# The opening of a streaming encoder layer in column halves: the scale's first half, then four chunks begun over half of the features

## The chip, the cores and the metric

One NeuronCore of a Trainium2 chip runs the whole program. The metric is the device time of one launch in microseconds. PE is TensorE, DVE VectorE, ACT ScalarE, POOL GpSimd, SP SyncE, whose queue issues nearly all large transfers.

## What is computed

One layer over 256 prompt tokens and 32 sample tokens of 1024 features, in float32. The scale and the shift come from a conditioning vector `c` of each of the two groups of tokens.

```python
sh1, sc1, g1, sh2, sc2, g2 = silu(c) @ w_ada + b_ada          # 6 x 1024 columns
h = rms_norm(x, norm1_g) * (1.0 + sc1) + sh1
proj = h @ w_in                                                # 512 pool, 512 conv value, 512 conv gate
a = pool_mix(proj[:512]);  u = proj[512:1024] * sigmoid(proj[1024:1536])
b = silu(layer_norm(depthwise_conv31(u))) @ conv_w_out
gates = sigmoid(h @ gate_w + gate_b)                           # 2048 columns
x = x + g1 * ((gates[:1024] * a + gates[1024:] * b) @ w_out)
h2 = rms_norm(x, norm2_g) * (1.0 + sc2) + sh2
x = x + g2 * moe_top4_of_32(h2)                                # three 1024x1024 matrices per expert
y = rms_norm(x, final_g)
```

## The kernel before

Each engine has one program written out by hand; semaphores order them. Nothing is scheduled by a planner: what stands earlier in an engine's text runs earlier.

**Weights of the front.** The list `FRONT` names pieces of 1 MB. SP issues them in that order (L454) into a ring of 12 slots; piece f waits for `piece_used` to reach f - 11, and PE counts that semaphore up when it has finished with a piece. The pieces in order are four of the scale, two of `w_in`, four of the shift, four more of `w_in`, then gates and the other modulation columns, and the pool, convolution and output weights. The three transfers of the tokens go ahead of all; the last of them is issued at 1.70 us.

**The opening.** `x` is squared on ACT in three tiles (L629), the root is taken (L632), DVE scales the tiles (L856), PE transposes them feature block by feature block (L1362, `turn_x`, eight in all) and DVE copies each block of 128 features to `hS` (L859). Beside it PE computes the modulation: `first_rows` (L1331) puts the bias into a bank, `first_half` (L1341) multiplies one piece, that is two feature blocks by all 1024 columns, in four products of 512 columns. Each of these takes 32 partitions of the bank, that is one strip of 32 columns of the array. ACT copies the finished bank to `rows` (L634), `to_columns` (L1352) turns it to columns, DVE makes `scc` and multiplies `hS` by it (L888). `fill` (L1320) is a product of the identity with ones whose result is never read.

**Projection.** It has 12 chunks of 128 columns, each a sum over 8 feature blocks (L1423, 128x288). The first four (`UNSHIFTED`) are taken before the shift is known: two of the convolution's gate and two of its value. The shift's own products (L1445) are added to their banks afterwards (L1464, through `group_of`), and `hT` (L900) is the shifted input of all others. In L1451 to L1459 the taps and the stored rows are transposed. Two gate and two value chunks are enough for tiles 0 and 1 of the depthwise convolution, which DVE runs as 31 taps per tile (L918 forms the product, L929 and L932 are the taps).

**Gates and after.** 16 gate chunks (L1476) alternate with products of the remaining modulation columns (L1397). The layer norm's mean and variance are taken in after gate chunks 6 and 8 (`MEAN_AT`, `VAR_AT`). Then pool, convolution and output products follow (L1526, L1546, L1563), and the router.

**Experts.** SP loads each expert in six pairs of slots (2 MB each); nine pairs are filled ahead, the last of them once `h2` is ready, and from the tenth on a load waits until PE is done with the pair it replaces (L493, issued in L460). An item is up to 64 tokens of one expert; 33 items run in this profile. An item begins with the gate product (L1690), 16 products that each stand as two records in the trace. Ahead of the first item PE passes the router's tables and two `fill(1)` calls.

## Time and profile before

| | |
|---|---|
| median of three runs | 1157.67 us (1156.29 to 1159.33) |
| profiled execution | 1158.99 us, its span 1157.1 us |
| PE busy | 1128.9 us (98%) |
| DVE busy | 500.3 us (43%) |
| ACT busy | 177.5 us (15%) |
| DMA share of 16 engines, ring and expert weights | 94.4% |
| HBM read | 454.40 MB, 394 GB/s over the span |

The profiled execution takes 1.9 us more than its span, for what lies around the recorded instructions. Busy time of PE is modelled and says little of how well it is used. The chain of work that ended last is followed back from the last instruction; its pieces are printed in order of time with start and length, so a piece that starts where the one before it ends leaves no hole. Clock is shown as a share of 2.4 GHz, so 0.50 is 1.2 GHz.

### The profile page before, as it was taken

The numbers are of one execution on the slowest core, as the hardware profiler recorded it, in microseconds if no ns is written. First come the engines' busy times: TensorE is split into PE (matmuls) and PEld (weight loads), VectorE is DVE, ScalarE is ACT, GpSimd is POOL, SyncE is SP. The second block draws the span as 40 slices with busy tenths as digits, with TensorE's granted clock in tenths as the row PEclk, the third lists the DMA queues.
The fourth block names the chain that finished last, engine by engine and source line by source line (L and its number), as shares of the span: only waits on it lengthen the run. The fifth ranks groups of instructions, "written<-read, shape, count | busy, mean of one in ns | idle before, by whom it ended". The sixth has DMA issues, their size and how long they took to land.

```text
span 1157.1 us, 16132 instructions
## 1 busy us (share of the span) xinstructions
PE 1128.9 (98%) x5964; PEld 459.7 (40%) x5965; DVE 500.3 (43%) x1143; ACT 177.5 (15%) x333; POOL 29.5 (3%) x78
## 2 busy tenths in 40 slices
PE   9999999999999999999999999999999999999996
PEld 6676675633333333333322333333333333333332
DVE  3398524654333443344333443344334433333334
ACT  2001301311111111111111112111111111111112
POOL 4002300000000000000000000000000000000000
PEclk9999999999999999999999999999999999999998
DMA  9977699699999999999999999999999999999994
GB/s 348 373 278 273 251 299 321 217 368 428 428 428 428 428 430 428 428 428 430 428 428 428 429 428 428 428 429 428 429 427 429 428 429 429 428 427 429 428 428 195
DMA packets 58012, 456.13 MB, mean 394 GB/s; under 512 B 7125, under 2 KB 26385, under 8 KB 31237
## 3 DMA queue, kind: packets, MB, share of 16 engines
q1 hardware_dynamic: 53872, 452.35, 94.4%
q10 hardware_dynamic: 4117, 3.47, 1.3%
q8 instruction: 16, 0.26, 0.1%
q14 instruction: 7, 0.06, 0.0%
HBM read 454.40 MB, written 1.40 MB: 394 GB/s over the span
## 4 chain that ended last, share of the span: by engine, by line
PE 78%; DMA 21%; DVE 1%; issue 0%; POOL 0%; DVEq 0%; SPq 0%; POOLq 0%
PE bank L1690 46%; DMA ring<-in_exp_w_up 7%; DMA ring<-in_exp_w_gate 7%; PE bank L1476 5%; PE bank L1423 4%; PE bank L1717 4%; PE bank L1642 4%; DMA arena<-in_exp_w_up 3%; DMA arena<-in_exp_w_gate 3%; PE bank L1563 2%; PE bank L1772 1%; PE bank L1546 1%; PE bank L1650 1%; PE bank L1397 1%; PE bank L1708 1%; PE bank L1320 1%
## 5 line engine op out<-in xcount | busy, mean ns | idle before, releaser
L1690 PE MATMUL bank<-ring,arena 128*64 128x512 f32 x2112 | 472.5, 598 | 11.3 <-DMA ring<-in_exp_w_gate 10.1
L1690 PEld LDWEIGHTS bank<-ring,arena 128*64 128x64 f32 x2112 | 146.9, 137 | 313.6 <-issue 286.5
L1690 PE MATMUL bank<-arena 128*64 128x512 f32 x1056 | 236.1, 595 | 5.3 <-DMA arena<-in_exp_w_gate 5.1
L1690 PEld LDWEIGHTS bank<-arena 128*64 128x64 f32 x1056 | 73.3, 137 | 155.5 <-issue 137.9
L780 ACT ACTIVATE arena<-arena 32x256 f32<-32x256 f32 x136 | 56.0, 412 | 422.8 <-DVE arena L1163 421.6
L1247 DVE TENSOR_SCALAR arena<-bank 128x512 f32<-128x512 f32 x33 | 22.8, 691 | 168.0 <-PE bank L1690 168.0
L1254 DVE TENSOR_SCALAR arena<-bank 128x512 f32<-128x512 f32 x33 | 22.8, 691 | 167.8 <-PE bank L1690 167.8
L1232 DVE TENSOR_TENSOR x<-x,bank 128x512 f32<-128x512 f32 x132 | 84.5, 681 | 13.0 <-PE bank L1717 13.0
L1269 DVE TENSOR_TENSOR arena<-bank,biases 128x512 f32<-128x512 f32 x66 | 42.5, 685 | 110.2 <-PE bank L1690 110.2
L793 ACT ACTIVATE arena<-arena 128x512 f32<-128x512 f32 x33 | 20.8, 629 | 356.7 <-DVE arena L1247 356.7
L1717 PE MATMUL bank<-arena 64*128 64x512 f32 x264 | 65.6, 615 | 0.0
L1476 PE MATMUL bank<-arena,ring 128*128 128x288 f32 x256 | 64.4, 409 | 0.0
L1642 PE MATMUL bank<-h,arena 128*64 128x512 f32 x268 | 63.3, 592 | 0.0
L932 DVE SCALAR_TENSOR_TENSOR h<-h,arena 128x318 f32<-128x318 f32 x120 | 55.5, 537 | 0.0
L1476 PEld LDWEIGHTS bank<-arena,ring 128*128 128x128 f32 x256 | 48.1, 190 | 17.1 <-issue 4.2
L1423 PE MATMUL bank<-arena,ring 128*128 128x288 f32 x192 | 47.7, 408 | 0.0
L793 ACT ACT_TABLE_LOAD x33 | 42.3, 1283 | 0.6
L1423 PEld LDWEIGHTS bank<-arena,ring 128*128 128x128 f32 x192 | 36.1, 190 | 11.4 <-issue 1.7
L1654 PE MATMUL bank<-biases,mine 32*64 32x288 f32 x264 | 40.0, 414 | 0.0
L1717 PEld LDWEIGHTS bank<-arena 64*128 64x128 f32 x264 | 22.7, 186 | 42.3 <-issue 42.3
L1168 DVE COPY arena<-arena 32x256 f32<-32x256 f32 x136 | 38.4, 282 | 2.5
L1651 PE MATMUL bank<-biases,mine 32*64 32x512 f32 x136 | 37.4, 613 | 0.0
(306 smaller groups left out, 742.8 us busy)
## 6 DMA issues: line engine op xcount, KB each, us to landing
ring<-in_exp_w_down SPq DMA_DIRECT2D x43, 2048.0 KB, 28.9
ring<-in_exp_w_up SPq DMA_DIRECT2D x43, 2048.0 KB, 28.8
ring<-in_exp_w_gate SPq DMA_DIRECT2D x42, 2048.0 KB, 28.1
arena<-in_exp_w_gate SPq DMA_DIRECT2D x22, 2048.0 KB, 26.4
arena<-in_exp_w_up SPq DMA_DIRECT2D x21, 2048.0 KB, 28.7
arena<-in_exp_w_down SPq DMA_DIRECT2D x20, 2048.0 KB, 30.3
ring<-in_w_ada SPq DMA_DIRECT2D x24, 1024.0 KB, 9.9
ring<-in_gate_w SPq DMA_DIRECT2D x8, 1024.0 KB, 7.8
```

What stands on the lines that cost most here:

```text
L780: ins = a.activation(*square_moves(1, s, u), ACT.Copy)
L793: a.activation(gsig, gmin, ACT.Sigmoid, scale=ALPHA).then_inc(gsig_ready, 1)
L932: ins = v.scalar_tensor_tensor(out=yc[:, c, :], in0=uc_ext[:, c, k:k + CW], scalar=tap, in1=yc[:, c, :], op0=ALU.mult, op1=ALU.add)
L1168: ins = v.tensor_copy(*square_moves(0, s, u))
L1232: ins = v.tensor_tensor(x[:, t, cs], x[:, t, cs], scatter_bank(t, hh), ALU.add)
L1269: v.tensor_tensor(ysb[:, gg, :], bank[5][:, :], g2h[:, gg, :], ALU.mult).then_inc(y_ev, 1)
L1423: ins = mm(bank[n % 4][:, 0:TOK], w[:, k, P * (n % 2):P * (n % 2 + 1)], (hS if n < UNSHIFTED else hT)[:, k, :], start=(k == 0), stop=(n >= ...
L1476: ins = mm(bank[n % 4][:, 0:TOK], w[:, k, P * (n % 2):P * (n % 2 + 1)], hT[:, k, :], start=(k == 0), stop=(k == KD - 1))
L1642: ins = mm(bank[0][64 * hh:64 * hh + 64, :], oh[:, t, :], half_rows(h2[:, t, :], hh), start=start, stop=stop, skip_group_check=True)
L1654: found = mm(bank[6 + i][out, 0:TOK], mine[LOOKUP, :], routedT[:, i, :], start=True, stop=True, skip_group_check=True)
L1690: ins = mm(out[64 * hh:64 * hh + 64, :], lhs(k), w[:, D * (k % 2) + HALF * hh:D * (k % 2) + HALF * (hh + 1)], start=(done is y_mm and k == ...
L1717: ins = mm(scatter_bank(t, hh), ohwT[64 * hh:64 * hh + 64, P * t:P * (t + 1)], ysb[64 * hh:64 * hh + 64, 0, :], start=True, stop=True, ski ...
```

## The change

**Pieces.** A scale or shift piece is now four feature blocks by 512 columns, named (kind, half of the columns, half of the features). A `w_in` piece is four feature blocks by 512 columns, so two pieces hold four chunks. The order is: both pieces of the scale's first 512 columns, the first `w_in` piece, the two of the scale's second half, the second `w_in` piece, four of the shift, four of `w_in`.

**Tokens.** ACT squares tiles 0 and 1 before anything else, DVE squares and sums tile 2 (32 rows). Then ACT scales tile 1 and DVE tiles 0 and 2. The sigmoid of `c` comes after that on ACT, with its table.

**PE.** The first four blocks of the tokens are transposed before any modulation product. The first scale half is made, turned to columns and applied to features 0 to 511. Then the four unshifted chunks, all gates of the convolution now, run over those features, with the second scale half between them; then the same four run over the other features, with the shift between them. Each half has its own bank (4 and 5), its own `first_rows` and its own `to_columns`. ACT copies blocks 4 to 7 to `hS` where DVE did.

**Later.** Chunk 4 is the first that gives the convolution a value. Taps run six alone for tile 0, then six for tile 1 (`ALONE`), then both in turn as before. `MEAN_AT` and `VAR_AT` go from 6 and 8 to 8 and 10; the modulation rows leave after gate 11 for 9, and two small copies on DVE move up. The two fills ahead of the first item become `fill(2)` and `fill(5)`.

```diff
-FRONT = ([("scale", 0, j) for j in range(4)] + [("in", c, 0) for c in (4, 2)]
-         + [("shift", 0, j) for j in range(4)] + [("in", c, 0) for c in (5, 3, 0, 1)]
+FRONT = ([("scale", 0, 0), ("scale", 0, 1), ("in", 2, 0), ("scale", 1, 0), ("scale", 1, 1), ("in", 2, 1)]
+         + [("shift", h, j) for h in range(2) for j in range(2)] + [("in", c, j) for c in (1, 0) for j in range(2)]
...
-MEAN_AT, VAR_AT, STATES_AT = 6, 8, 10
+MEAN_AT, VAR_AT, STATES_AT = 8, 10, 10
...
+            a.activation(stat[:, 31:32], stat[:, 30:31], ACT.Sqrt)
+            for t in range(2):
+                act.wait_ge(x_ld[t], 16)
+                a.activation(view(2304 + D * t, D), x[:, t, :], ACT.Square, accum_out=stat[:, t:t + 1]).then_inc(ssq, 1)
+            act.wait_ge(mean2, 1)
+            a.activation(stat[:, 4:7], stat[:, 8:11], ACT.Sqrt).then_inc(sqrt_ready, 1)
+            act.wait_ge(rstd0_ready, 1)
+            a.activation(h2[:, 1, :], x[:, 1, :], ACT.Copy, scale=stat[:, 5:6]).then_inc(xn_ready, 1)
             act.wait_ge(c_cols_ready, 1)
             a.activation(csig[:, :], c_cols[:, :], ACT.Sigmoid).then_inc(csig_ready, 1)
...
+            for k in range(4, KD):
+                act.wait_ge(xT, k + 1)
+                a.activation(hS[:, k, :], bank[k % 4][:, 0:TOK], ACT.Copy).then_inc(xT_act, 1)
...
+            dve.wait_ge(x_ld[2], 16)
+            step(v.tensor_tensor(squares, x[0:NS_TOK, 2, :], x[0:NS_TOK, 2, :], ALU.mult))
+            step(v.tensor_reduce(stat[0:NS_TOK, 2:3], squares, AX, ALU.add))
...
-            glu((0, 1))
+            glu((0,))
+            dve.wait_ge(u_ready, 1)
+            dve.wait_ge(dw_ready, 1)
+            conv((0,), 0, ALONE)
+            glu((1,))
             dve.wait_ge(u_ready, 2)
-            dve.wait_ge(dw_ready, 1)
-            conv((0, 1), 0, CONV_SPLIT)
+            conv((1,), 0, ALONE)
+            conv((0, 1), ALONE, CONV_SPLIT)
...
-            first_rows(2)
-            fill(3)
-            pe.wait_ge(cT_ready, 1)
-            fill(4)
-            first_half("scale", 0)
-            fill(6)
-            first_half("scale", 1)
+            first_rows(2, bank[4])
+            fill(12)
+            pe.wait_ge(xn_ready, TT)
+            for k in range(4):
+                turn_x(k)
...
+            pe.wait_ge(cT_ready, 1)
+            first_half("scale", 0, 0)
+            first_half("scale", 0, 1)
             turn_x(4)
-            fill(2)
-            first_half("scale", 3)
             turn_x(5)
+            pe.wait_ge(pick_made, 2)
+            to_columns(0, 0)
             turn_x(6)
-            pe.wait_ge(pick_made, 2)
-            to_columns(0)
             turn_x(7)
+            pe.wait_ge(cols_ready, 1)
+            first_rows(3, bank[5])
             fill(2)
...
+            for n in range(UNSHIFTED):
+                pe.wait_ge(xT_act, n + 1)
+                chunk(n, 0)
+                if n < 2:
+                    first_half("scale", 1, n)
+                elif n == 2:
+                    to_columns(0, 1)
+            first_rows(0, bank[4])
+            first_rows(1, bank[5])
+            for n in range(UNSHIFTED):
+                chunk(n, 1)
+                first_half("shift", n // 2, n % 2)
+                if n == 3:
+                    to_columns(1, 0)
+                    to_columns(1, 1)
+
+            pe.wait_ge(shift_ready, 2)
...
-            fill(1, bank[1])
+            fill(2, bank[1])
             pe.wait_ge(begun_ready, 1)
...
-            fill(1, bank[1])
+            fill(5, bank[1])
             pe.wait_ge(base_ready, 1)
```

How the order of instructions moves, at two places. First PE, from the last fill ahead of the first projection chunk: before, whole chunks in a row.

```order
L1320 MATMUL bank<-ones,ident 128x128 x2
L1423 MATMUL bank<-arena,ring 128x288 x16
L1331 MATMUL bank<-arena 32x512 x2
L1341 MATMUL bank<-ring,cT 32x512 x8
L1423 MATMUL bank<-arena,ring 128x288 x8
L1341 MATMUL bank<-ring,cT 32x512 x8
L1423 MATMUL bank<-arena,ring 128x288 x4
L1352 MATMUL bank<-arena 128x4 x4
L1423 MATMUL bank<-arena,ring 128x288 x4
L1445 MATMUL bank<-ring,arena 32x256 x16
```

The same place with the change (`first_rows` is now L1341, `first_half` L1348, `to_columns` L1360, the chunks L1417):

```order
L1341 MATMUL bank<-arena 32x512
L1331 MATMUL bank<-ones,ident 128x128 x2
L1417 MATMUL bank<-arena,ring 128x288 x4
L1348 MATMUL bank<-ring,cT 32x512 x4
L1417 MATMUL bank<-arena,ring 128x288 x4
L1348 MATMUL bank<-ring,cT 32x512 x4
L1417 MATMUL bank<-arena,ring 128x288 x4
L1360 MATMUL bank<-arena 128x4 x4
L1417 MATMUL bank<-arena,ring 128x288 x4
L1341 MATMUL bank<-arena 32x512 x2
L1417 MATMUL bank<-arena,ring 128x288 x4
L1348 MATMUL bank<-ring,cT 32x512 x4
```

Four products, half a chunk, now stand between pieces of the modulation, columns are turned between them, and the bias row of the scale's second half stands ahead of the first chunk.

Second DVE, where the depthwise convolution starts: before, both tiles' products first, then the taps of both in turn.

```order
L918 TENSOR_TENSOR h<-bank,arena 128x256
L918 TENSOR_TENSOR h<-bank,arena 128x32
L918 TENSOR_TENSOR h<-bank,arena 128x256
L918 TENSOR_TENSOR h<-bank,arena 128x32
L929 TENSOR_SCALAR h<-h,arena,cols 128x318 x2
L932 SCALAR_TENSOR_TENSOR h<-h,arena 128x318 x34
```

The same place with the change (L924 forms the product, L935 and L938 are the taps):

```order
L924 TENSOR_TENSOR h<-bank,arena 128x256
L924 TENSOR_TENSOR h<-bank,arena 128x32
L935 TENSOR_SCALAR h<-h,arena,cols 128x318
L938 SCALAR_TENSOR_TENSOR h<-h,arena 128x318 x5
L924 TENSOR_TENSOR h<-bank,arena 128x256
L924 TENSOR_TENSOR h<-bank,arena 128x32
L935 TENSOR_SCALAR h<-h,arena,cols 128x318
L938 SCALAR_TENSOR_TENSOR h<-h,arena 128x318 x29
```

Tile 0 now has its product and six taps (one in L935, five in L938) ahead of tile 1's product.

## Rows read from the trace of the kernel before

**Rows 1.** The page, section 4: shares of the chain that ended last

```profile
PE 78%; DMA 21%; DVE 1%; issue 0%; POOL 0%; DVEq 0%; SPq 0%; POOLq 0%
```

**Rows 2.** The chain in order of time, opening: start us, us, what

```profile
13.76 0.99 PE bank L1341 x8
...
15.81 2.02 PE bank L1362 x12
...
22.09 0.98 PE bank L1352 x8
...
23.52 0.64 PE bank L1320 x4
24.17 7.87 PE bank L1423 x32
32.04 0.98 PE bank L1331 x4
33.01 1.85 PE bank L1341 x16
34.87 4.08 PE bank L1423 x16
...
40.80 2.14 PE bank L1423 x8
42.94 0.79 PE bank L1352 x8
43.72 2.05 PE bank L1423 x8
45.77 1.86 PE bank L1445 x32
...
48.49 2.14 PE bank L1464 x8
```

**Rows 3.** The chain of the whole program: chunks, first item, late experts

```profile
50.63 31.04 PE bank L1423 x128
...
230.85 9.79 PE bank L1690 x32
...
243.12 7.02 PE bank L1690 x32
...
1001.72 40.33 DMA ring<-in_exp_w_up
```

**Rows 4.** Windows: length, PE, PEld, DVE, ACT, POOL busy, PEclk, DMA share, GB/s

```profile
230.00:231.00 1.00, 0.23 (x3) 0.16 (x4) 0.88 (x5) 0.96 (x3) 0.00 (x0) 0.50 1.07 459
...
237.00:238.00 1.00, 1.00 (x8) 0.39 (x6) 0.24 (x3) 0.00 (x0) 0.00 (x0) 1.00 0.04 16
```

**Rows 5.** Timeline of SP's queue: start us, us, engine, line, transfer

```profile
237.24 0.33 SPq L460 DMA_DIRECT2D ring<-in_exp_w_up  x1
```

**Rows 6.** Timeline of the opening, ACT and DVE; last row: landing of the tokens

```profile
4.24 1.28 ACT L623 ACT_TABLE_LOAD   x1 [4.24 <-issue]
...
8.03 1.04 ACT L629 ACTIVATE arena<-x 128x1024 f32<-128x1024 f32 x1
...
11.27 0.17 DVE L835 TENSOR_SCALAR stat<-stat 128x3 f32<-128x3 f32 x1 [4.45 <-ACT arena L629]
...
11.92 2.07 DVE L856 TENSOR_SCALAR h<-x,stat 128x1024 f32<-128x1024 f32 x3
...
DMA to landing us min/median/max: 3.3/4.6/5.3
```

**Rows 7.** Timeline of DVE, later: a reduce and a product of 1024 columns

```profile
109.00 2.39 DVE L947 TENSOR_REDUCE arena<-h 128x318 f32<-128x1272 f32 x1
...
202.02 1.21 DVE L1051 TENSOR_TENSOR h<-h,arena 32x1024 f32<-32x1024 f32 x1
```

**Rows 8.** Timeline of DVE where the convolution begins

```profile
50.35 0.95 DVE L918 TENSOR_TENSOR h<-bank,arena 128x256 f32<-128x256 f32 x4 [2.03 <-ACT arena L659]
...
52.05 8.37 DVE L932 SCALAR_TENSOR_TENSOR h<-h,arena 128x318 f32<-128x318 f32 x18
```

More of the change, by code:

```diff
@@ L419, in build @@
         ada_piece = {(a, b): f for f, (kind, a, b) in enumerate(FRONT) if kind == "ada"}
+        piece_of = {piece: f for f, piece in enumerate(FRONT)}
         pool_stage = [biases[0:POOL_PAD, 0, 0:DC], biases[0:CONV_PAD, 0, DC:D]]
@@ L637, in _ @@
             act.dma_start(dw_stage, conv_dw[0]).then_inc(dw_ld, 16)
+            act.wait_ge(ada_mm, 2)
+            a.activation(rows[:, 1, :], bank[5][:, :], ACT.Copy).then_inc(rows_ready, 1)
             act.dma_start(pool_stage[0], state_pool[0, 0]).then_inc(st_ld, 16)
             act.dma_start(pool_stage[1], state_conv[0, 0]).then_inc(st_ld, 16)
-            act.wait_ge(ada_mm, 2)
-            a.activation(rows[:, 1, :], bank[4][:, :], ACT.Copy).then_inc(rows_ready, 1)
+            act.wait_ge(ada_mm, 3)
@@ L642, in _ @@
+            a.activation(rows[:, 0, :], bank[4][:, :], ACT.Copy).then_inc(rows_ready, 1)
+            act.wait_ge(ada_mm, 4)
+            a.activation(rows[:, 1, :], bank[5][:, :], ACT.Copy).then_inc(rows_ready, 1)
             act.wait_ge(shift_mm, 1)
@@ L866, in _ @@
+            scale_half(0)
+            scale_half(1)
+            v.memset(uc_ext[:, :, 0:CONV_PAD], 0.0).then_inc(hist0_ready, 1)
             dve.wait_ge(const, 7)
             v.reciprocal(invc[:, :, :], invc[:, :, :]).then_inc(mod_ready, 1)
-            def columns(at):
-                return bank[7][:, at:at + 16].rearrange("p (r j g) -> p j r g", r=4, j=2)
-            four = "p (j r g) -> p j r g"
-            dve.wait_ge(modT, 1)
-            for gg in range(2):
-                v.scalar_tensor_tensor(out=scc[:, :].rearrange(four, j=2, g=2)[:, :, :, gg], in0=columns(0)[:, :, :, gg],
-                                       scalar=1.0, in1=cols[:, C_N1:C_N1 + KD].rearrange("p (j r) -> p j r", j=2),
-                                       op0=ALU.add, op1=ALU.mult).then_inc(mod_ready, 1)
@@ new lines, in _ @@
+            pe.wait_ge(shift_ready, 2)
+            for k in range(KD):
+                q = k % 4
+                ins = mm(bank[4][32 * q:32 * q + 32, :], shT[:, k, :], front_piece(piece_of[("in", 2, k // 4)])[1][:, k % 4, :],
+                         start=(k < 4), stop=(k >= 4), skip_group_check=True)
+            ins.then_inc(shift_mm, 1)
+            pe.wait_ge(cols_ready, 1)
+            pe.wait_ge(dw_ld, 16)
+            for c in range(CT):
+                ins = tr(bank[5][:, 32 * c:32 * c + WIDTH], dw_stage[:, P * c:P * (c + 1)], ident[0:WIDTH, 0:WIDTH])
+                if c == 0:
+                    ins.then_inc(piece_used, 8)
@@ new lines, in _ @@
+            ins.then_inc(dwT, 1)
+            pe.wait_ge(st_ld, 32)
+            for c in range(CT):
+                tr(bank[6][:, 32 * c:32 * c + POOL_PAD], pool_stage[0][:, P * c:P * (c + 1)], ident[0:POOL_PAD, 0:POOL_PAD])
+            for c in range(CT):
+                ins = tr(bank[6][:, 128 + 32 * c:128 + 32 * c + CONV_PAD], pool_stage[1][:, P * c:P * (c + 1)],
+                         ident[0:CONV_PAD, 0:CONV_PAD])
+            ins.then_inc(stT, 1)
+            pe.wait_ge(shift_ev, 1)
@@ L1467, in _ @@
+            for m in range(UNSHIFTED):
+                mm(bank[m][:, 0:TOK], rows[:, 2, P * m:P * (m + 1)], group_of, start=False, stop=True,
+                   skip_group_check=True).then_inc(in_mm, 1)
+            for n in range(UNSHIFTED, 12):
+                if n < 8:
+                    pe.wait_ge(sig_ready, n - 3)
+                else:
+                    pe.wait_ge(u_ready, n - 7)
+                chunk(n, 0)
+                chunk(n, 1).then_inc(in_mm, 1)
             for n in range(2 * KD):
```

244 lines of the change are left out of this document (91 added, 153 removed).

## Prediction, made before the changed kernel ran

> **What bounds the kernel now.** I read the page's shares of the chain first, then the chain in order of time, then clock and DMA in short windows, then DVE and ACT where the change touches them.
>
> The page gives 78% of the chain that ended last to PE and 21% to DMA [rows 1]. In order of time these are two regimes. From 13.76 us on the chain is PE without a hole: each piece starts where the one before it ends, and the eight projection chunks from 50.63 on take 31.04 us in one piece [rows 2, 3]. Where PE had to wait, small identity products ("fills") stand in the chain, as at 23.52, so a wait there reads as PE work. In the second regime, the experts, the chain ends in DMA: one weight half ends 40.33 us of it [rows 3]. The two are tied. Nine pairs of slots are filled ahead, and the tenth transfer waits until the first item has used pair 0. So the end comes a fixed stream of transfers after that first use, unless the DMA engines are still busy with the pairs ahead. They just weren't: their traffic fell to 16 GB/s at 237 to 238 us, and the tenth transfer was issued at 237.24 [rows 4, 5].
>
> Hence: what the opening gains or loses on PE arrives at the first item, and from there at the end, nearly one to one. The sum is made against the profiled execution, 1158.99 us; the median of the three runs is 1157.67, so that execution lies 1.32 above it. A measurement of this kernel can tell about 0.3%, here 3.5 us, from no change: faster means under 1154.2, slower over 1161.1.
>
> **When the tokens' transposes can start.** Before: the normalised tokens were there at 11.92 + 2.07 = 14.0, but PE, with two scale pieces ahead of them, came at 15.81 [rows 2, 6]. Now ACT loads its root table first (1.28 from 4.24) and squares two tiles, 1.04 each [rows 6]: 5.5, its root of one element 0.2, then 5.75 to about 8.05. DVE squares the third tile once it has landed, 1.70 + 5.3 = 7.0 [rows 6]. The square costs 1.21 by the row of a 32x1024 operation; the sum of 1024 elements I bound by that row and by the 2.39 of the reduce over 1272 elements [rows 7], and take 1.5, since it has fewer elements and reads them in order: 9.8. From mean to first scaled tile took 11.92 - 11.27 = 0.65 [rows 6]; two tiles remain on DVE, 2 x 0.7, ACT does the third beside them. That gives 11.9 to 12.8; I take **12.5**, 3.3 earlier than 15.81.
>
> **PE from there to the fifth chunk.** Terms, with the rows of group 2:
> - Eight transposed blocks 2 x 2.02 (four at 15.81) = 4.1 with the sum's rounding up, the small table 0.2: as before.
> - The first scale half, two pieces together as 1.85, was half done before the transposes and is now behind them.
> - Columns of the scale: 0.98. The bias row of the other half, a lone 512-column product: the row at 32.04 has two in 0.98, but in different column strips of the array, and four in four strips also take 0.99 (13.76). So 0.98 is the time of one, not of two. Bounds 0.49 and 0.98; I take 0.9. Two fills 0.3 each.
> - First chunk at 12.5 + 4.1 + 0.2 + 1.85 + 0.98 + 0.9 + 0.6 = **21.1**, against 24.17. Its cover is good: the row copy on ACT (0.6) lies beside two transposes.
> - Eight half chunks at 2.1 (2.14 at 40.80) = 16.8; before, the four chunks took 7.87 + 4.08 + 2.14 + 2.05 = 16.1, as a product that follows another kind pays some 0.15.
> - Six pieces one at a time 6 x 0.99 = 5.9, where four stood in pairs (1.85 each).
> - Columns again 0.8, and twice in a row 1.7 (0.79 to 0.98 each): there are four such steps where there were two.
> - Two bias rows, now in two banks but the same strip: 1.8, where they were side by side in 0.98.
> - The wait for the shift's columns, until now covered by half a chunk (43.72 stands behind 42.94), is open: copies on DVE, 0.4.
> - Shift products 1.86 (eight of 512 for sixteen of 256), stored rows and taps 48.49 - 47.63 = 0.86, shift added 2.14: as before.
>
> 21.1 + 16.8 + 5.9 + 0.8 + 1.7 + 1.8 + 0.4 + 1.86 + 0.86 + 2.14 = **53.4**, against 50.63: **2.8 later**. The first chunk comes 3 us sooner, and the path behind it has grown by nearly 6, two of them the second scale half that is carried past it, the rest steps that are now split, repeated or uncovered.
>
> **DVE.** The convolution began beside chunk four (50.35, [rows 8]) because its two operands were among the first four chunks. Now all four first chunks are gates, so it begins 3.9 + 0.3 after chunk four starts. Tile 0 alone takes six taps, each waiting for the last: 5 x 0.6 + 0.4; the same for tile 1; then 24 at 8.37 / 18 = 0.465 [rows 8]. The third product is ready 23.6 after the chunk began, and chunk ten, which needs its bank, could start at 6 x 3.88 = 23.3 (3.88 is 31.04 / 8). I charge **0.4**. Everything behind comes some 7 us later relative to PE; the mean and the variance were moved two gates later each (about 10 us), which covers it, and the activation for the output is then due some 12 us after it is ready. Cost nothing.
>
> **DMA.** The ring's early releases are now later and coarser: two before the taps' transposes, then eight at once. After the tokens (7.0 us) 14 pieces of 1.05 MB take 37 us at the page's 394 GB/s; then the queue is dry from 44 to the taps' transposes at 50.4, some 6 us. The first gate piece is needed 31 us later and takes a few: nothing. The weight pieces arrive before PE asks for them, since PE asks later.
>
> **The clock at the first item.** Ahead of 230.85 PE has only the small products of the router's tables, two single fills and a gap (busy 0.23 of the window from 230); the granted clock has fallen to 0.50 there, 1.2 GHz, and reads 1.00 again from 237 [rows 4]. The first product takes 9.79, the next like it 7.02 [rows 3]. Pair 0 comes free half a product in, at 16 x 0.4 instead of 16 x 0.22 us: 2.9 late, of which the idle DMA shows 2.0, and a half us more at the next transfers. The change raises these two fills to two and five, five more, 5 x 0.3 = 1.5 us by the two of them in 0.64 [rows 2]. Bounds of the gain: 0 (clock falls all the same) and 2.5 (stays up); against the gain at most 0.3, as the next work queues behind them. Taken: 2.2 gained, 0.2 paid, because the five stand exactly where the fall began.
> The Trainium skill (TensorE: Matmul & The Clock Gate, section "Why this matters for your kernels") asks that PE not be left idle between bursts. By that rule alone nothing here asked for a fall, since the gap is under 1 us, and more fills would give nothing: the end would be 1162.4. The trace differs: the clock fell.
>
> Sum: 1158.99 + 2.8 + 0.4 + 0.2 - 2.2 = **1160.2 us**.
>
> **Rivals.**
> - *The clock falls all the same.* Place: the first product of the first item. For it: the router's small products stay as they are, and more fills may not hold the clock. Price: 2.2 back, 1162.4, slower. It decides as soon as less than 1.3 of the 2.2 is won. Chance 0.33.
> - *PE's list is not additive.* The 0.15 at each change of kind, the lone bias rows and the extra column steps may slip beside their neighbours, as weight loads do. Then the half chunks cost 15.7, bias rows 1.5 in all, columns 0.5 each: 53.4 - 1.1 - 1.2 - 1.5 = 49.6, and the end is 1156.4. For it: PE is never idle in rows whose busy time is modelled. Against it: the same switches in the rows of before all cost this. Chance 0.17; a third of it, with a first use earlier than the pairs' landing and a short reduce, goes below 1154.2.
> - *The tokens come late.* If squares or landing of the third tile drag (reduce 2.39, tile at 8), transposes start at 14 and PE idles 1.5 before them: 1161.7, and with a clock that falls in that hole, 2 more. Chance 0.1.
> - *The half-column order does not matter*, since the steps taken up by fills before are merely renamed and the fifth chunk starts at 50.6 again: 1157.4. Chance 0.05.
>
> **Numbers.** Forecast 0.35, clock 0.33, the others as given. Below 1154.2 lie a third of the second rival's 0.17 and 0.02 of the forecast's own spread (1158.5 to 1162): 0.08. Over 1161.1 lie 0.27 of the clock's case, 0.07 of the late tokens' and 0.06 of that spread: 0.4; between, 0.52. The range takes in the clock's case and 0.9 us above it, 1163.3, and below it the second rival's 1156.4 and 0.4 more: 1156.0.
>
> **What would show it.** First half chunk at 21 (right if 20.5 to 22), first of the eight unbroken chunks at 53.4 (52.4 to 54.4), bias rows about 1.8 for two, the first item at 234. Windows behind it: clock near 1.00 and first product near 7. The second rival's case shows the fifth chunk before 51. I am wrong in kind if PE waits for a weight piece anywhere before 230, if DVE holds chunk ten by more than 1 us or the gates at all, or if the end does not follow the first item.

## The result, and the profile after

The change made the kernel slower by about half a per cent: 1162.88 us, median of 8 runs (1161.26 to 1165.71), against 1157.74 for the kernel before in the same job (8 runs, 1154.32 to 1159.33). The ratio is 1.0053 with a 95% interval of 1.0041 to 1.0064. The forecast was 1160.2, within 0.3% of before; the time lies inside the range, at its upper end, and outside "same".

The profiled execution of the changed kernel took 1161.58 us, its span is 1159.6. The shares of the chain that ended last, page section 4, answer to [rows 1] and hardly moved:

```profile
PE 76%; DMA 21%; DVE 2%; issue 0%; ACTq 0%; DVEq 0%; SPq 0%
```

The two points of DVE are new. The chain in order of time (start us, us, what) answers to [rows 2, 3] and shows where they come from (`...` marks pieces left out):

```profile
8.29 4.29 PE bank L1331 x24
12.59 2.02 PE bank L1370 x12
...
17.74 0.99 PE bank L1360 x8
...
19.71 0.97 PE bank L1341 x2
...
21.33 3.59 PE bank L1417 x8
24.92 1.00 PE bank L1348 x8
25.91 2.14 PE bank L1417 x8
...
34.02 1.83 PE bank L1341 x4
...
48.38 1.89 PE bank L1360 x16
...
50.39 0.17 DVE arena L900
...
50.61 1.92 PE bank L1442 x16
...
53.39 2.14 PE bank L1461 x8
55.52 3.89 PE bank L1417 x16
...
78.92 8.03 PE bank L1417 x32
86.95 7.76 PE bank L1481 x32
...
234.87 1.31 PE bank L1331 x10
...
236.28 7.09 PE bank L1695 x32
```

The transposes start at 12.59, 3.2 earlier than before, and the first half chunk at 21.33, 2.8 earlier. From there the path is longer: the fifth chunk starts at 55.52, 4.9 later than before. The first half chunk takes 3.59 where every later one takes 2.14 or 2.05. Chunk ten waits for the convolution on DVE (the chain runs over DVE from 59.4 to 78.9), so the gate stage follows the start of the fifth chunk after 31.43 us and not 31.04.

The windows (length, PE, PEld, DVE, ACT, POOL busy, granted clock, DMA share, GB/s) give the reason for the 3.59 and show the place of [rows 4]:

```profile
22.00:23.00 1.00, 1.00 (x4) 0.71 (x3) 0.00 (x0) 0.00 (x0) 0.00 (x0) 0.50 1.04 383
23.00:24.00 1.00, 1.00 (x3) 0.71 (x3) 0.00 (x0) 0.00 (x0) 0.00 (x0) 0.50 1.05 389
...
25.00:26.00 1.00, 1.00 (x9) 0.16 (x3) 0.00 (x0) 0.00 (x0) 0.00 (x0) 1.00 1.04 375
...
236.00:237.00 1.00, 0.90 (x6) 0.35 (x6) 0.86 (x5) 0.98 (x3) 0.00 (x0) 1.00 1.12 475
237.00:238.00 1.00, 1.00 (x6) 0.30 (x4) 0.85 (x5) 0.98 (x1) 0.00 (x0) 1.00 0.96 410
```

The clock was at its lower level, 1.2 GHz, from about 21.5 to 24.9, straight behind the transposes, pieces and columns, although PE's rows show it busy throughout 19 to 25. At the first item it now stays at 1.00, and DMA has no gap: 410 GB/s at 237 to 238, where [rows 4] have 16. The tenth transfer was issued at 239.97, against 237.24 in [rows 5]:

```profile
239.97 0.33 SPq L463 DMA_DIRECT2D ring<-in_exp_w_up  x1
```

From that issue to the end of the span it is 919.6 us here and 919.9 before. So the profiled difference is settled at this point: 2.7 later, 2.6 longer.

One thing at the very start the windows don't show. They print 1.00 for all time ahead of the trace's first clock record, and that record lies at 11.2 us here and at 11.1 in the kernel before, but at 4.9 to 6.2 in the profiles of e2, e4, e5, e7, e8, e9, e11 and e12 below. Ahead of it PE's rows take about twice as long: a lone bias row 1.91 at 6.38 against 0.97 at 19.71, and the twelve fills from 8.29 on 4.29 against some 2.9 in those eight. So PE presumably ran at the lower level until then, and when that ends differs between executions. It decides here when the fills end and the transposes begin.

The tokens, on DVE and ACT, which answer to [rows 6, 7]:

```profile
7.22 1.21 DVE L847 TENSOR_TENSOR arena<-x 32x1024 f32<-32x1024 f32 x1 [0.86 <-DMA x<-in_x_sample]
...
8.46 1.21 DVE L848 TENSOR_REDUCE stat<-arena 32x1 f32<-32x1024 f32 x1
...
10.36 1.15 ACT L633 ACTIVATE h<-x,stat 128x1024 f32<-128x1024 f32 x1 [0.24 <-DVE stat L852]
10.36 1.40 DVE L856 TENSOR_SCALAR h<-x,stat 128x1024 f32<-128x1024 f32 x2
```

### The profile page after: what moved, and what is told of

Same layout as the page of the kernel before. It is cut to its first block, busy times and chain, and to the rows that moved or that the text cites. A ratio compares the mean times of both kernels' runs of the same rounds, so it can differ in the third digit from the quotient of the medians.

```text
span 1159.6 us, 16138 instructions
## 1 busy us (share of the span) xinstructions
PE 1131.6 (98%) x5962; PEld 460.5 (40%) x5963; DVE 501.3 (43%) x1142; ACT 178.9 (15%) x336; POOL 30.3 (3%) x80
## 4 chain that ended last, share of the span: by engine, by line
PE 76%; DMA 21%; DVE 2%; issue 0%; ACTq 0%; DVEq 0%; SPq 0%
PE bank L1695 45%; DMA ring<-in_exp_w_up 7%; DMA ring<-in_exp_w_gate 7%; PE bank L1481 5%; PE bank L1722 4%; PE bank L1647 4%; DMA arena<-in_exp_w_up 3%; DMA arena<-in_exp_w_gate 3%; PE bank L1417 3%; PE bank L1568 2%; PE bank L1777 1%; DVE h L938 1%; PE bank L1551 1%; PE bank L1655 1%; PE bank L1401 1%; PE bank L1713 1%
## 5 line engine op out<-in xcount | busy, mean ns | idle before, releaser
L1243 DVE TENSOR_TENSOR x<-x,bank 128x512 f32<-128x512 f32 x132 | 84.5, 681 | 12.6 <-PE bank L1722 12.6
L1481 PE MATMUL bank<-arena,ring 128*128 128x288 f32 x256 | 64.4, 409 | 0.0
L938 DVE SCALAR_TENSOR_TENSOR h<-h,arena 128x318 f32<-128x318 f32 x120 | 56.3, 536 | 0.4
L1417 PE MATMUL bank<-arena,ring 128*128 128x288 f32 x192 | 50.7, 420 | 0.1
L1417 PEld LDWEIGHTS bank<-arena,ring 128*128 128x128 f32 x192 | 36.6, 194 | 15.2 <-issue 5.0
L1661 PE MATMUL bank<-h,arena 32*64 32x512 f32 x136 | 37.4, 613 | 0.0
```

Source lines behind the costliest of these rows:

```text
L938: ins = v.scalar_tensor_tensor(out=yc[:, c, :], in0=uc_ext[:, c, k:k + CW], scalar=tap, in1=yc[:, c, :], op0=ALU.mult, op1=ALU.add)
L1243: ins = v.tensor_tensor(x[:, t, cs], x[:, t, cs], scatter_bank(t, hh), ALU.add)
L1417: ins = mm(bank[n % 4][:, 0:TOK], w[:, k % 4, P * (n % 4):P * (n % 4 + 1)], (hS if n < UNSHIFTED else hT)[:, k, :], start=(k == 0), stop=( ...
L1481: ins = mm(bank[n % 4][:, 0:TOK], w[:, k, P * (n % 2):P * (n % 2 + 1)], hT[:, k, :], start=(k == 0), stop=(k == KD - 1))
```

## What was to be told apart

Profile against profile the change cost 2.6 us. The clock in one half chunk is 1.65 of it: the first half chunk took 3.59, and 1.94 at full clock (e2, e10 and e11 below). The medians are 5.1 apart: the profiled execution of before lay 1.3 above its median and that of after 1.3 below. Two theories:

- **A.** The list of steps on PE is priced rightly, and the rest is the clock: the new opening puts small products in longer stretches, with waits of PE among them, and loses the clock there in many executions. The mean granted clock of a run tells how long it was down after the first clock record: 0.001 of 1160 us is 2.3 us at half speed, or 1.2 us of PE's work not done.
- **B.** The list is dear in itself (column steps, bias rows, single pieces), and the clock is a detail of one execution.

Each kernel below ran in 5 rounds beside the kernel before, and its ratio to that is what counts: the median of before was 1156.45 in the first job of e1 to e4, 1157.64 for e5 to e8, 1157.57 for e9 and e10, 1158.2 for e11 and e12.

## The fills ahead of the first item

**e1, the kernel before with the two fill counts of the change, nothing else.**

```diff
-            fill(1, bank[1])
+            fill(2, bank[1])
...
-            fill(1, bank[1])
+            fill(5, bank[1])
```

> The kernel before with only the last edit of the change: two and five fills ahead of the first item instead of one and one. Theory (the fills hold the clock at the first item): the first product takes about 7.1 us instead of 9.79, the tenth weight transfer is issued some 2.7 us sooner, and the median is 1 to 2.5 us under that of the kernel before. Rival (the clock at the first item is chance, the fills do nothing): first product near 9.8 or 7 by luck, median within 0.5 us of before.

**e2, the change with these fills put back to one each** (the same diff the other way).

> The changed kernel with one and one fill again. Theory: the first product is near 9.8 us again with a granted clock of 0.50 at it, and the median rises by 1 to 2.5 us over the changed kernel's 1162.9. Rival: no difference, 1162.9 within 0.5.

Measured: e1 1154.94 (12 runs), ratio 0.9987 [0.9977, 0.9997]; e2 1164.85 (6 runs), 1.0084 [1.0061, 1.0106]. The first item in the chain of e1, and below it in that of e2:

```profile
232.40 7.09 PE bank L1690 x32
```

```profile
236.79 8.78 PE bank L1695 x32
```

The clock in e2's windows there:

```profile
236.00:238.00 2.00, 1.21 (x4) 0.45 (x6) 1.79 (x9) 1.95 (x5) 0.00 (x0) 0.75 0.96 410
238.00:240.00 2.00, 2.00 (x6) 0.51 (x4) 1.73 (x10) 0.92 (x1) 0.00 (x0) 0.50 1.07 459
```

With seven fills the first product took 7.09 in eleven of the twelve profiles that have them; with two it took 9.79 (before) and 8.78 (e2, where the clock fell only as the product began). The twelfth is e8, below: its clock was down from 238.3 to 251.9 in spite of seven fills.

```profile
248.93 8.52 PE bank L1691 x32
```

So the fills make the fall there rare, not impossible. They are the one part of the change that was seen to gain over the kernel before: 1.5 us by e1's median and ratio, and 2.0 (medians) to 3.6 (ratios) between e2 and the change. So the opening by itself costs more than the result shows: 1.0053 / 0.9987 is 1.0066, 7.6 us, and e2, which is the opening without the fills, measured 1.0084, 9.7 us, with an interval that takes in both.

e1 also shows scatter that the mean clock doesn't tell. Its twelve runs all read 0.997 or 0.998 and spread over 3.3 us. In its profile the fifth chunk started at 51.89, 1.26 later than in that of before, with the windows at 1.00 in both; the first clock record lay at 13.8 instead of 11.1, and the pieces before it took up to twice as long.

## Parts of the opening

**e3, bias rows of the two halves in two strips of the array.**

```diff
-                mm(out[0:32, :], ada_sel[:, row, :], bada[:, :], start=True, stop=False, skip_group_check=True)
+                mm(out[32 * (row % 2):32 * (row % 2) + 32, :], ada_sel[:, row, :], bada[:, :], start=True, stop=False, skip_group_check=True)
...
-                             start=(j == 0 and q > 0), stop=(j == 1), skip_group_check=True)
+                             start=(j == 0 and q != h), stop=(j == 1), skip_group_check=True)
```

> The changed kernel, but the bias row of each second half goes to the second strip of 32 partitions instead of the first, so that the two bias rows of the shift stand in different strips. Theory (a lone 512-column product takes as long as four in four strips, and two in one strip are serial): the pair takes 0.98 us instead of 1.83, everything behind comes 0.85 sooner, median 1162.0. Rival (the pair is bound by its bank or its issue): still 1.8, median unchanged.

Measured: 1164.16 (6 runs), 1.0078 [1.0058, 1.0099]. The pair of bias rows in the chain of e3:

```profile
33.80 0.98 PE bank L1341 x4
```

1.83 has become 0.98, and the fifth chunk of the profiled execution starts 1.06 earlier, at 54.46; that execution took 1160.19. The median didn't follow. The six runs are spread over 1160.19 to 1168.83, with clocks from 0.987 to 0.996: the 0.85 is real in the profile, and lost in the scatter of the clock.

**e4, the token blocks turned by products with the identity instead of transposes.** Values are the same.

```diff
-                    ins = tr(bank[k % 4][:, P * t:P * t + r], h2[0:r, t, P * k:P * (k + 1)], ident[0:r, 0:r])
+                    ins = mm(bank[k % 4][:, P * t:P * t + r], h2[0:r, t, P * k:P * (k + 1)], ident[0:r, 0:r], start=True, stop=True)
```

> The changed kernel with the 24 transposes of the tokens made as ordinary products with the identity. It tests what lets the clock fall at the first half chunk (0.50 from 21.7 to 24.9 us in the changed kernel's profile). Theory A (transposes do not hold the clock): the clock stays at 1.00 through the first half chunk, which takes 2.1 us instead of 3.59; median 1.5 us lower if that happens in most runs. Theory B (it is the thin products, four columns and four rows, between them, or where the clock's own rhythm falls): 3.6 again, or 2.1 with no change of the median. If a product costs more than a transpose, the eight blocks take over 4.1 us.

Measured: 1169.42 (5 runs), 1.0112 [1.0092, 1.0133]. Chain, then a window, of e4:

```profile
11.55 6.08 PE bank L1370 x24
```

```profile
13.00:15.00 2.00, 2.00 (x10) 1.71 (x8) 0.64 (x3) 0.00 (x0) 1.48 (x8) 0.50 1.06 389
```

Twice the records, at half clock: 6.08 for what took 2.02. So the fall isn't bound to transposes as a kind. Real products of this size, with PE busy 2.00 of 2.00 us, stood in it from 12.7 to 22.9, and the clock was down again from 26.3 to 33.2. But PE had waited 1.6 us for the tokens just ahead of these products, so this execution alone doesn't tell the wait from the products.

**e5, the last two token blocks turned later, each behind a half chunk.**

```diff
-            turn_x(6)
-            turn_x(7)
...
                 if n < 2:
+                    turn_x(6 + n)
                     first_half("scale", 1, n)
```

> The changed kernel with the last two transposed blocks moved from ahead of the first half chunk to behind the first and the second one. Nothing is added. Theory (after the half-column order PE has 4.7 us of transposes, four-column products and a lone bias row in one stretch, and there the clock falls): the stretch is 3.7 us, the first half chunk starts 1 us sooner (about 20.3), the start of chunk four gains little (the blocks cost the same behind it), but falls are rarer: mean granted clock of the runs over the changed kernel's 0.9946 mean, median about 1 us lower. Rival (falls come by the clock's own rhythm, wherever PE is): clock and median as in the changed kernel.

Measured: 1163.58 (6 runs), 1.0075 [1.0047, 1.0103]. Chain of e5:

```profile
19.93 3.56 PE bank L1415 x8
...
49.96 3.29 PE bank L1441 x16
```

The first half chunk comes 1.4 sooner, half of it because the transposes began 0.7 sooner, and is as slow as in the change. A second place appears: the shift products took 3.29 instead of 1.92. One microsecond less of small work ahead of the chunk did not keep the clock, and the mean clock of the runs came out lower than the change's, 0.992, where the theory had it higher.

**e6, two wide products (128 x 512) in the stretch, one of them for the two last fills.**

```diff
+            def wide():
+
+                mm(bank[6][:, :], ident[:, :], ring[:, 1, 0:HALF], start=True, stop=True)
+
...
+            wide()
             to_columns(0, 0)
...
-            fill(2)
+            wide()
```

> The changed kernel with a full 128x128 by 512 product whose result is not read put behind the sixth transposed block, and another in the place of the two short fills before the first half chunk. Cost by the list: 0.85 + 0.25 = 1.1 us of PE ahead of the first half chunk (it starts at about 22.4). Theory (long products hold the clock): no fall at the first half chunk, it takes 2.1 us instead of 3.59; the granted clock of the runs reads 0.997 or so and they scatter by less; median equal to the changed kernel's or up to 1 us lower. Rival: falls as before, median 1.1 us higher.

Measured: 1164.57 (6 runs), 1.0066 [1.005, 1.0083]. Chain, then a window, of e6:

```profile
21.19 2.00 PE bank L1366 x2
23.20 2.64 PE bank L1422 x8
```

```profile
22.00:24.00 2.00, 2.00 (x5) 1.06 (x4) 0.00 (x0) 0.00 (x0) 0.00 (x0) 0.50 1.05 385
```

The fall came all the same: the first wide product took 1.06, the second, at the lower clock, 2.00. They did not keep the clock, and the mean clock is that of the change (0.9947 for 0.9946). Their own time is 1.7 us by the medians, for 1.1 expected, though the intervals of the two ratios overlap.

**e8, the tokens handled as before (sigmoid first, all squares on ACT, all scaling on DVE), with the new order on PE.** The part on the squares:

```diff
-            for t in range(2):
+            for t in range(TT):
+                r = ROWS[t]
                 act.wait_ge(x_ld[t], 16)
...
-            step(v.tensor_tensor(squares, x[0:NS_TOK, 2, :], x[0:NS_TOK, 2, :], ALU.mult))
-            step(v.tensor_reduce(stat[0:NS_TOK, 2:3], squares, AX, ALU.add))
```

> The changed kernel with the tokens handled as before: sigmoid first, all three tiles squared on ACT, all three scaled on DVE; PE's order unchanged. Theory (the transposes start when the scaled tokens are there): they start at about 14.2 instead of 12.6, and PE is idle between its fills and then; everything behind is 1.6 us later plus what a fall of the clock in that hole costs; median 1164.5 to 1167. Rival (pieces of the scale bound the opening, so the tokens' order is hidden): within 0.5 us of the changed kernel.

**e10, e8 with 17 fills for 12 ahead of the transposes.**

> The version with the tokens' squares back on ACT (e8), whose transposes stood at half clock from 14.04 on, with 17 fills instead of 12 ahead of the transposes, so that the time from 12.6 to 14.0 in which PE waited for the tokens is filled. Theory A (that idle time dropped the clock, and the late tokens by themselves cost only 1.5 us): transposes from about 14.1 at full clock (x12 in 2.0, not 3.5), first half chunk at 22.7 to 23.5, median 1164 to 1166 (ratio 1.005 to 1.007). Theory B (the thin work from 12 to 22 us loses the clock whether PE waited before it or not): transposes 3.5 again, first half chunk after 28, median near e8's 1169.

Measured: e8 1169.26 (6 runs), 1.0094 [1.0069, 1.012]; e10 1163.97 (6 runs), 1.0061 [1.0042, 1.0081]. e8 is over the 1164.5 to 1167 that were expected, and its profiled execution, 1175.65, is the slowest of its six. PE's timeline of e8 (in brackets the wait ahead and what ended it), then a window:

```profile
7.31 2.94 PE L1327 MATMUL bank<-ones,ident 128*128 128x128 f32 x24
14.04 3.51 PE L1366 MATMUL bank<-ident,h 128*128 128x128 f32 x12 [3.79 <-DVE h L858]
```

```profile
16.00:22.00 6.00, 6.00 (x26) 1.82 (x25) 1.35 (x4) 0.55 (x1) 1.04 (x4) 0.50 1.05 387
```

The same places in e10, windows and chain:

```profile
12.00:14.00 2.00, 2.00 (x12) 2.00 (x12) 1.99 (x3) 0.00 (x0) 1.86 (x2) 1.00 1.05 387
...
16.00:22.00 6.00, 6.00 (x43) 3.35 (x43) 2.17 (x10) 1.86 (x5) 1.05 (x4) 1.00 1.05 387
```

```profile
14.72 2.02 PE bank L1366 x12
```

Five small fills gave back 5.3 us by the medians, 3.8 by the ratios, whose intervals overlap. Between the two profiles the first half chunk starts 6.1 us sooner, at 23.47 instead of 29.53, although the transposes began 0.7 later. In e8 PE stood idle from 10.25 to 14.04, 3.8 us and not the 1.4 that the expectation of e10 names; the clock fell at 13.0, inside this wait, and stayed at 1.2 GHz for 20.5 us. In e10 there was no wait. Part of this is the start again: e10's first clock record lies at 13.7, and its 17 fills took 6.74. At the pace of e8's fills they would end some 2.5 us before the tokens (estimate: 34 records at 2.94 / 24), so the five fills don't close the wait in every execution; the mean clock of the six, 0.9962 for 0.989, is what says that they mostly work. This is the strongest effect of the study. Filled, the late tokens cost little: e10's ratio is 0.0008 over that of the change, 0.9 us, and the two intervals overlap.

The other half of the distance between these two profiles, 5.4 of 11.8 us, arose between the gate stage and the tenth transfer, where e8 lost the clock a second time (238.3 to 251.9). Whether the late tokens had a part in that is not shown.

## A leaner list, and the second place

**e7, all of it together:** strips as e3, late blocks as e5, the bias row and the small tables moved to where nothing waits for them, and the convolution's taps in turn end at 16 instead of 18.

```diff
-ALONE, CONV_SPLIT = 6, 18
+ALONE, CONV_SPLIT = 6, 16
...
             for k in range(4):
                 turn_x(k)
+            first_rows(3, bank[5])
...
-            to_columns(0, 0)
-            turn_x(6)
-            turn_x(7)
             pe.wait_ge(cols_ready, 1)
-            first_rows(3, bank[5])
+            to_columns(0, 0)
```

> The changed kernel with four costs of its opening taken away: the late two transposed blocks of the other run, the scale's second bias row made at the start beside the first (0.97 off the path), the shift's two bias rows in different strips (0.85), and 16 instead of 18 taps ahead of the second pair of products (0.4, the hold of the eleventh chunk, goes). Theory (PE's list is additive): chunk four starts 1.8 us sooner than with the same clock, 2.2 in all at the first item; against the changed kernel's profile of 1161.58 that is 1159.4, or 1157.8 if the clock does not fall at the first half chunk. The kernel before with its better fills, 1154.9, still is not reached. Rival (the list is not additive, waits for pieces or the tokens come in): less than 1 us gained.

Measured: 1159.06 (12 runs), 1.0021 [1.001, 1.0032]. Its chain:

```profile
18.34 2.18 PE bank L1415 x8
...
30.41 0.98 PE bank L1341 x4
...
46.14 3.41 PE bank L1441 x16
...
52.68 31.04 PE bank L1415 x128
```

3.8 us less than the change, by the medians and between the two profiles; the steps that were taken out sum to 2.2. The profiles tell where the 3.8 are: 1.64 because the transposes began sooner (10.95, first clock record at 5.5), 1.20 between them and the fifth chunk, 0.39 for the hold of chunk ten (the eight chunks are in one piece of 31.04 again), 0.56 behind the tenth transfer. Of the 1.82 expected up to the fifth chunk (bias row 0.97, strips 0.85), 1.2 came, with about the same loss by the clock in both (1.65 in the half chunk there, 1.63 at the shift here): with the bias row and two blocks gone, PE waited 0.49 for the scaled features. So the list is additive until such a wait opens, and that the profile met the 1157.8 expected for a kept clock (1157.78) is luck. The shift products stood at half clock, directly behind PE's wait for the columns. Two edits of that place:

**e9, the two column steps of the shift with half of a half chunk behind each.** The new third argument of `chunk` picks feature blocks.

```diff
             for n in range(UNSHIFTED):
-                chunk(n, 1)
+                if n < 3:
+                    chunk(n, 1)
                 first_half("shift", n // 2, n % 2)
-                if n == 3:
-                    to_columns(1, 0)
-                    to_columns(1, 1)
+            to_columns(1, 0)
+            chunk(3, 1, slice(0, 2))
+            to_columns(1, 1)
+            chunk(3, 1, slice(2, 4))
```

> The leaner version (e7) with one more edit: the last half chunk (four gate chunks' last, 2.14 us) is cut in two and put between the two column steps of the shift, the last shift piece before them. Nothing is added. The wait for the shift's column copies (0.34) is covered again, so the gate chunks should start 0.3 to 0.5 earlier relative to the first half chunk (65.4 after it in e7's profile, so 64.9 to 65.1), less if the clock falls. Theory A (the clock falls at about 46 to 53 us because last piece, two column steps, shift products, transposes of taps and states stand in one stretch of small products, some 7 us long, and before that there was a half chunk inside it): the shift products take 1.9 instead of 3.4, the mean clock of all runs rises from e7's 0.9956 to 0.997 or more, and the median is 1.5 to 2.5 under e7's (ratio to before about 0.999 to 1.001). Theory B (the falls come with time and chance and are not bound to that stretch): the median is 0.3 to 0.5 under e7's (ratio 1.001 to 1.002) and the shift products take 3.4 in the profile again.

**e12, e7 with three fills ahead of the wait.**

```diff
+            fill(3)
             pe.wait_ge(shift_ready, 2)
```

> The leaner version (e7) with three fills ahead of the wait for the shift's column copies, where PE stood for 0.35, and nothing else: the stretch of small products stays as long as in e7. Theory A (the wait decides): shift products 1.9 instead of 3.4 in the profile, fifth chunk 1.5 to 2 earlier than in e7 relative to the first half chunk (34.3 there, so 32.3 to 32.9), median 1 to 1.5 under e7's (ratio 1.0005 to 1.001), as e9. Theory B (the length of the stretch decides): shift products 3.4 again, median e7's or up to 0.3 over it (ratio 1.002 to 1.0025).

Measured: e9 1158.05 (12 runs), 1.0007 [0.9994, 1.002]; e12 1158.86 (12 runs), 1.001 [1.0, 1.0021]. Chain of e9, then of e12:

```profile
18.45 3.71 PE bank L1415 x8
...
47.37 1.85 PE bank L1443 x16
```

```profile
18.45 3.48 PE bank L1415 x8
...
47.48 0.77 PE bank L1331 x6
48.25 1.85 PE bank L1442 x16
```

In both the shift products take 1.85. In e12 the stretch of small products is as long as in e7, and longer by the fills; only the wait is gone. That speaks for the wait and against the length. The times don't decide it: by ratio the gain on e7 is 1.6 and 1.3 us (e12 by medians only 0.2), but the intervals overlap e7's, and e9's mean clock, 0.9957, did not rise to the 0.997 that its theory A asked for. The evidence is in the profiles. Nine of the changed kernels have the wait open (0.35): in the change, e3 and e8 the shift products kept their 1.92, in six they took 2.51 (e2), 2.65 (e4), 3.29 (e5), 3.44 (e6), 3.41 (e7) and 3.54 (e10). The three with the wait covered or filled (e9, e12 and e11, below) all took 1.85. Were the six falls spread over the twelve profiles by chance, those three would be free of one in 20 of 220 cases, 9%. Before and e1, whose wait is covered by half a chunk, kept 1.86 as well. I take it that the wait matters, and that it makes the fall likely, not certain; it is made likely here, not shown. The first half chunk, 2.18 in e7, was slow in both e9 and e12.

**e11, e9 with six fills for two between the scale's columns and the first half chunk,** where PE waited about 0.5.

```diff
             to_columns(0, 0)
-            fill(2)
+            fill(6)
```

> The version with split column steps (e9) with six fills instead of two between the scale's columns and the first half chunk, where PE waited some 0.5 us for the scaled features. Theory A (a wait of PE ahead of the first half chunk decides whether the clock stays up): the first half chunk takes 2.2 at full clock, first half chunk still starts about 7.4 after the transposes, the fifth chunk at about 51, median 1155.5 to 1157 (ratio 0.998 to 1.000) with a mean clock of 0.997 or more. Theory B (the small products before it decide, filled or not): the first half chunk takes 3.5 to 3.7 in some executions as before, mean clock 0.9955 to 0.996, median within 0.7 of e9's 1158 (ratio 1.000 to 1.0015).

Measured: 1158.25 (12 runs), 1.0012 [0.9998, 1.0027]. Its chain:

```profile
14.99 3.57 PE bank L1348 x16
...
22.27 1.94 PE bank L1415 x8
```

The half chunk is fast, as theory A of that run had it, but here the clock had fallen earlier, and the median is that of e9. Its windows:

```profile
10.00:12.00 2.00, 0.47 (x3) 0.30 (x3) 1.44 (x3) 1.91 (x2) 1.64 (x4) 1.00 1.06 392
12.00:14.00 2.00, 2.00 (x8) 1.17 (x9) 1.20 (x4) 0.74 (x2) 1.55 (x7) 0.53 1.05 385
```

PE waited 1.84 us for the tokens, from 9.70 on, and the clock fell at 12.1, with the transposes under way. The same wait was 1.07 to 1.23 in e9, e12, e7 and e5 and 1.79 in e2, and the clock stayed up through the transposes behind it; behind 1.61 in e4 and 1.84 here, and inside 3.79 in e8, it fell. So longer waits went with the fall, and 1.61 against 1.79 shows that the length alone doesn't decide. Filling the wait ahead of the half chunk settled nothing about that place: the fall moves about in the opening from one execution to the next, and twelve fills end before the tokens come in the eight executions whose first clock record is early. The first half chunk or the transposes ahead of it were slow in the profiles of the change, e3, e4, e5, e6, e8, e9, e11 and e12, and at full clock in e2, e7 and e10. In the change, e3 and e6 PE had no wait over 0.25 us between 7 us and the fall, and in e5 none just before it. What decides at this place stays open.

The mean clock of all runs of a kernel, beside the ratio:

| kernel | mean clock | ratio to before |
|---|---|---|
| before | 0.995 to 0.996 | 1 |
| e1, fills alone | 0.9974 | 0.9987 |
| the change | 0.9946 | 1.0053 |
| e2, fills back | 0.9905 | 1.0084 |
| e3, e5 | 0.992 | 1.0078, 1.0075 |
| e4, e8 | 0.991, 0.989 | 1.0112, 1.0094 |
| e6 | 0.9947 | 1.0066 |
| e10 | 0.9962 | 1.0061 |
| e7, e9 | 0.9956, 0.9957 | 1.0021, 1.0007 |
| e11, e12 | 0.9961, 0.9968 | 1.0012, 1.001 |

Neither theory alone makes this table. e10 keeps the clock and is slow; e3 has a shorter list than the change and is not faster, with a lower clock. Within one kernel the time follows the clock at about the price of theory A: the change's two runs at 0.993 took 1164.59 and 1165.71, its two at 0.996 took 1161.26 and 1161.58; e8's six go from 1164.07 at 0.995 to 1175.65 at 0.984. An estimate of the parts of the opening's 7.6 us: the change has 0.0028 less clock than e1, 3.2 us at that price, and some 4.4 are the list. The profiles agree roughly on the list: 4.9 at the fifth chunk less 1.65, and 0.4 for chunk ten, is 3.6.

## Why the prediction was wrong, step by step

**Tokens: the number right, by luck.** Transposes at 12.59 for 12.5. But what set it was not the tokens: they were scaled at 11.76, below the forecast's 11.9 to 12.8, and PE came out of its twelve fills at 12.6, since these ran slowly ahead of the first clock record. Where the fills ended sooner the tokens did set it, at 10.95 to 11.89 (e2, e4, e5, e7, e9, e11, e12), behind a wait of PE that the prediction had only as a rival for late tokens. The reduce took 1.21 for an estimate of 1.5.

**PE up to the first chunk: right.** 21.33 for 21.1, a lone bias row 0.97 for 0.9.

**The steps from there: right in the list, wrong in the clock.** The fifth chunk was forecast at 53.4 and came at 55.52. Bias pair 1.83 for 1.8, the wait 0.34 for 0.4, pieces 5.97 for 5.9, shift products 1.92 for 1.86, column pair 1.89 for 1.7. The step that failed is "Eight half chunks at 2.1 (2.14 at 40.80) = 16.8": they took 18.5. At full clock the first takes 1.94 (e2, e10, e11), and with that the eight sum to 16.8, just as forecast. So the 1.65 are the first one's half clock, a cost that the sum put at nothing. The rows of before had no fall between its first clock record and the fifth chunk, and I carried their durations into a list with longer stretches of small work and a newly open wait, without asking whether the clock would stay. The prediction looked at the clock only at the first item. That the clock fell is shown; why it fell at this place is open, as said above.

**The rival that the list is not additive: wrong in the main.** It had the fifth chunk at 49.6. The rows carry the single prices of the sum, and e3 gave back the 0.85 of a strip in full; e7 gave 1.2 of 1.8, because a wait opened.

**Chunk ten: right.** 31.43 - 31.04 = 0.39, charged 0.4; e7 removes it.

**DMA: right where it counts.** The queue is dry for longer than said (0.05 of the DMA engines busy from 45 to 54, where I had 6 us), and PE never waits for a weight piece in the chain of the front.

**The first item: right between the profiles, less in the medians.** First product 7.09. Between the gate stage and the tenth transfer the change is 2.5 us shorter than before (153.0 against 155.6), where I had 2.0 net, and e1 is 2.4 shorter. The median of e1 gained only 1.5; the fastest runs of before, 1153.5 to 1154.5, have clocks of 0.997 and 0.998, so some of its executions may keep the clock there without the fills, which no profile shows.

**The end follows the first item: right,** 918.6 to 919.9 from the tenth transfer to the end in all fourteen profiles.

In sum: 1158.99 + 4.9 + 0.4 - 2.5 = 1161.8, measured 1161.58. The forecast for the profiled execution was 1.4 low: the half chunk put it 1.65 low and other small terms of the opening 0.5, and the first item and the end gave 0.8 back.

The median lies another 1.3 over the profile. By the runs' clocks (0.9946 on average, 0.996 in the profile, hence an estimate of 1.6 us) this is most likely more of the same in other executions: falls at the second place, or longer ones. That part is argued and not shown. Which executions they hit could not be seen, since only one of each kernel has a profile. And the baseline was set high: before's profiled execution, at a clock of 0.994 where its runs average 0.9952 to 0.9956, lies 1.3 above its median, which I said and did not use. Profile against profile the change is 0.22% slower, within what the prediction called no change; the medians make it 0.5%. That the median still fell inside the range owes something to luck: the range was held open upwards for a loss of clock at the first item, which did not come, and a loss in the opening took its place.

**A version that may beat both** is e1, the old opening with the new fills: 1154.94. Its gain over before, 0.13%, is below the 0.3% that a few runs can tell, though the interval from 12 and 17 runs just excludes 1. None of the reworked openings was faster than before; e9, with the same fills, comes level with it.

## What to carry over

Before adding up durations of rows for a new order, ask at what clock they will run: a place where the new order lets PE wait ahead of a stretch of small products may cost once as the wait, and again as what stands behind it at half speed (in e8's profile a wait of 3.8 us, and the first half chunk 6 us later than with the wait filled). Fill such a wait with small products and look at the windows' clock in more than one run, since the mean clock of the unprofiled runs tells part of what the one profile hides. And undo one part of a compound change: here its smallest part, five small products, was all of the gain that could be measured.

## What was not expected of the hardware

- The clock reads 0.50 while PE's rows are unbroken: 22 to 24 in the change, 13 to 22 in e4, 22 to 24 in e6 from the second wide product on. Busy rows alone did not keep it; a wait before them often, not always, went with the fall.
- A fall is not a property of the list alone: e7, e9 and e12 have the same list up to that point and nearly the same times up to 18 us, and the half chunk behind took 2.18, 3.71 and 3.48.
- The first clock record lies between 4.9 and 13.8 us in the fourteen profiles, and PE's rows ahead of it take about twice as long, while the windows print 1.00.
- Two 512-column products in one strip of 32 columns of the array took 1.83, in two strips 0.98, though they write different banks.
- The same kernel's mean clock differed between executions by up to 0.011 (e5 and e8), which is some 26 us at the lower level; the times of these executions differed by 9.9 us in e5 and 11.6 in e8.
